# First-half inverse roots moved to GpSimd as one power, and the per-layer-embedding stage's first-half squares added on VectorE

## The reference

```
def rmsnorm(x, g):
    xf = x.astype(jnp.float32)
    y = xf * lax.rsqrt(jnp.mean(xf * xf, axis=-1, keepdims=True) + EPS)
    return (y * g.astype(jnp.float32)).astype(x.dtype)
...
def conv_ffn(xn, w_up, conv_w, conv_b, w_down, prev):
    u = xn @ w_up
...
    return h @ w_down, up[:, -(CONV_W - 1):]

def ple_term(h, p, g, w_gate, w_proj):
    return jax.nn.sigmoid(rmsnorm(h, g) @ w_gate) * (p @ w_proj)
...
        hp = hp + rmsnorm(yp, g_post_mix[i])
        fp, cvp = conv_ffn(rmsnorm(hp, g_pre_ffn[i]), ffn_w_up[i], ffn_conv_w[i], ffn_conv_b[i], ffn_w_down[i],
                           jnp.zeros((Bp, CONV_W - 1, 2 * D_FF), hp.dtype))
        hp = hp + rmsnorm(fp, g_post_ffn[i])
        hp = hp + ple_term(hp, p_prompt[i], g_ple[i], ple_w_gate[i], ple_w_proj[i])
```

## Time and profile before

| | us |
|---|---|
| median of 3 runs | 1319.02 |
| lowest, highest | 1319.0, 1319.26 |
| the profiled execution | 1319.47 |
| its span | 1317.7 |
| TensorE busy | 1307.0 |
| VectorE busy | 856.8 |
| ScalarE busy | 583.8 |
| GpSimd busy | 67.8 |

### The profile page before, as it was taken

How to read it: one execution, slowest core, us unless ns; L and a number is a source line. 1 busy time by engine, 2 the same in 40 slices (tenths; PEclk the granted TensorE clock), 3 DMA queues, 4 the chain that set the end, 5 groups by cost and what they waited for, 6 DMA issues and landing times.

```text
span 1317.7 us, 25501 instructions
## 1 busy us (share of the span) xinstructions
PE 1307.0 (99%) x10944; PEld 1270.2 (96%) x10944; DVE 856.8 (65%) x1552; ACT 583.8 (44%) x1031; POOL 67.8 (5%) x102
## 2 busy tenths in 40 slices
PE   9999999999999999999999999999999999999998
PEld 7999989999999999999999987999999999999998
DVE  6437675887777775222887788698777777432385
ACT  5222345654444443222754768554444444222371
POOL 1110322000000000000013010000000000000000
PEclk9999999999999999999999999999999999999999
DMA  4542732213332233222414232221332233322231
GB/s 169 174 107 93 244 113 65 97 57 89 96 97 85 93 96 134 89 89 83 145 33 150 87 101 70 80 83 41 96 97 86 91 97 98 122 89 89 77 129 65
DMA packets 34802, 131.64 MB, mean 100 GB/s; under 512 B 4197, under 2 KB 4781, under 8 KB 34401
## 3 DMA queue, kind: packets, MB, share of 16 engines
q1 hardware_dynamic: 29376, 111.59, 26.2%
q0 software_dynamic: 5024, 18.05, 4.4%
q10 hardware_dynamic: 288, 0.37, 0.1%
HBM read 121.08 MB, written 10.05 MB: 100 GB/s over the span
## 4 chain that ended last, share of the span: by engine, by line
PE 94%; DVE 3%; ACT 1%; DMA 1%; issue 0%; SPq 0%; DVEq 0%; ACTq 0%
PE tile L1151 24%; PE tile L1155 24%; PE tile L1153 24%; PE tile L1161 4%; PE tile L1162 4%; PE tile L1163 4%; PE tile L1665 1%; PE side L1161 1%; DVE wL L1848 1%; DMA h<-in_x 1%; PE side L1162 1%; PE side L1163 1%; DVE cv L1881 0%; DVE cg L1853 0%; PE side L1323 0%
## 5 line engine op out<-in xcount | busy, mean ns | idle before, releaser
L734 ACT ACTIVATE wH<-raw 128x1024 fp32r<-128x1024 f32 (+1 forms) x191 | 212.0, 1112 | 379.7 <-DMA raw<-in_w_up 142.0
L1151 PE MATMUL tile<-xH,wH 128*128 128x260 f32 x1800 | 365.0, 284 | 2.5 <-DVE xL L1942 1.5
L1155 PE MATMUL tile<-xH,wL 128*128 128x260 f32 x1800 | 362.7, 283 | 0.0
L1153 PE MATMUL tile<-xL,wH 128*128 128x260 f32 x1800 | 362.2, 283 | 0.0
L1848 DVE TENSOR_TENSOR wL<-raw,wH 128x1024 fp32r<-128x1024 f32 (+1 forms) x191 | 248.1, 1300 | 152.1 <-ACT wH L734 147.9
L1151 PEld LDWEIGHTS tile<-xH,wH 128*128 128x128 f32 x1800 | 277.3, 189 | 6.7 <-DVE kvq L1896 2.6
L1155 PEld LDWEIGHTS tile<-xH,wL 128*128 128x128 f32 x1800 | 277.5, 188 | 0.0
L1153 PEld LDWEIGHTS tile<-xL,wH 128*128 128x128 f32 x1800 | 276.7, 188 | 0.0
L1896 DVE SCALAR_TENSOR_TENSOR u<-tile,rstd 128x520 f32<-128x520 f32 x96 | 67.2, 700 | 123.4 <-PE tile L1155 123.4
L1151 PE MATMUL tile<-hidH,wH 128*128 128x260 f32 x616 | 124.3, 283 | 0.0
L1155 PE MATMUL tile<-hidH,wL 128*128 128x260 f32 x616 | 123.8, 282 | 0.0
(11 more groups left out here) (461 smaller groups left out, 1895.1 us busy)
## 6 DMA issues: line engine op xcount, KB each, us to landing
raw<-in_w_up SPq DMA_DIRECT2D x88, 512.0 KB, 3.6
raw<-in_w_down SPq DMA_DIRECT2D x32, 704.0 KB, 4.1
raw<-in_w_ple SPq DMA_DIRECT2D x16, 512.0 KB, 5.7
raw<-in_w_qo SPq DMA_DIRECT2D x12, 512.0 KB, 3.5
raw<-in_w_qkv SPq DMA_DIRECT2D x12, 512.0 KB, 3.6
raw<-in_w_kv SPq DMA_DIRECT2D x11, 512.0 KB, 3.6
cring<-in_c_in POOLq DMA_DIRECT2D x8, 512.0 KB, 4.6
out_c_s<-cring POOLq DMA_DIRECT2D x8, 512.0 KB, 3.2
```

The costliest lines, as they stand in the source:

```text
L734: nc.scalar.activation(wH[j][:, 0:n], raw[j][:, 0:n], ACT.Copy).then_inc(s_high, 1)
L1151: nc.tensor.matmul(out[:, q, 0:HT], wh, x[0][:, k, tokens(q)], start=first, stop=False)
L1153: nc.tensor.matmul(out[:, q, 0:HT], wh, x[1][:, k, tokens(q)], start=False, stop=False)
L1155: mm = nc.tensor.matmul(out[:, q, 0:HT], wl, x[0][:, k, tokens(q)], start=False, stop=last)
```

## The change

There are three edits, in both layers.

1. For the first half of "up" and of "ple", ScalarE writes mean square plus epsilon (the identity in place of the root), and GpSimd raises it to the power -0.5 in place, against a one-column constant. VectorE's reciprocal of this half is gone; VectorE waits for GpSimd.
2. The first half of "ple" has no column groups: TensorE's two `square_group` calls and ScalarE's `group_sums` go. VectorE adds the 8 tiles of squares in four instructions (`fold_early`, `fold_late`), and `square_sum` moves from before the first halves to after the fifth k of the third one.
3. The order in "ple" follows: VectorE's three weight blocks stand earlier, ScalarE splits the third block before its third input of the second half, `pre_root` stands one input later, and TensorE's groups for the second half stand one k later.

```
-GROUPED = {sq: n + 1 for n, sq in enumerate(sq for sq in PREROOT if sq[0][:2] != "up" or sq[1])}
+GROUPED = {sq: n + 1 for n, sq in enumerate(sq for sq in PREROOT if sq[1])}
...
+            def inverse_root(stage):
+
+                pool.wait_ge(s_rinv, PREROOT[stage, 1] // 2)
+                pool.wait_ge(s_rootp, PREROOT[stage, 0])
+                nc.gpsimd.tensor_tensor(rstd[:, tokens(0)], rstd[:, tokens(0)], minus_half[:].to_broadcast([P, HT]), ALU.pow
+                                        ).then_inc(s_rinv, 1)
+
             for layer in range(NL):
...
                 nc.gpsimd.memset(u[:, :, 0:2], 0.0).then_inc(s_pad, 1)
+                inverse_root(up)
                 pool.wait_ge(s_hid, FT * (layer + 1))
                 pool.dma_start(g.newrows[layer], newrows[:]).then_inc(s_out, 16)
                 stored += 1
 
                 pool.dma_start(pin[:], g.p[layer]).then_inc(s_p, 16)
+                inverse_root(ple)
...
-                nc.scalar.activation(rstd[:, tokens(q)], sums[:, q, 0:HT], ACT.Sqrt, bias=eps[:, 0:1],
+                nc.scalar.activation(rstd[:, tokens(q)], sums[:, q, 0:HT], ACT.Sqrt if q else ACT.Identity, bias=eps[:, 0:1],
...
                 ple_input(0, 1)
-                group_sums(ple, 0)
                 high(ple, 1)
                 p_copy(6)
                 ple_input(1, 1)
                 p_copy(7)
+                high(ple, 2)
                 ple_input(2, 1)
+                ple_input(3, 1)
                 pre_root(ple, 0)
-                ple_input(3, 1)
-                high(ple, 2)
...
-                    if j == 2:
-                        square_group(ple, 0, 0)
-                    if j == 5:
-                        square_group(ple, 0, 1)
 
                 yd = YREAD0[down]
-                square_sum(ple, 0)
                 first_half(ple, 0, (s_yr, yd + KT - 1))
                 first_half(ple, 1, (s_pwr, 2 * KT * (layer + 1)))
-                first_half(ple, 2, (s_pwr, 2 * KT * (layer + 1)))
-                for k in range(3):
+                first_half(ple, 2, (s_pwr, 2 * KT * (layer + 1)), lambda k: square_sum(ple, 0) if k == 4 else None)
+                for k in range(4):
...
             def pre_one_over(stage, q):
+                if q == 0:
+                    dve.wait_ge(s_rinv, 1 + PREROOT[stage, 1] // 2)
+                    return
...
+            def fold_early(stage):
+
+                dve.wait_ge(s_sq, SQ0[stage] + KT // 2)
+                chain.did(nc.vector.tensor_tensor(sg[0], sg[0], sg[1], ALU.add))
+
+            def fold_late(stage):
+
+                dve.wait_ge(s_sq, SQ0[stage] + KT)
+                late = squares_ple[:, 0:KT // 2, :].rearrange("p n t -> p (n t)")
+                chain.link(nc.vector.tensor_tensor(late[:, 0:T], late[:, 0:T], late[:, T:2 * T], ALU.add))
+                chain.link(nc.vector.tensor_tensor(sg[0], sg[0], late[:, 0:T], ALU.add))
+                nc.vector.tensor_tensor(square(stage, 0, 0), square(stage, 0, 0), square(stage, 0, 1), ALU.add).then_inc(s_fold, 1)
...
+                    if k == KT:
+                        fold_early(ple)
                 one_over(down, 1, cg[:, tokens(1)])
+                low(ple, 0)
                 for k in range(KT + 2):
                     step(k, 1)
-                    if k in (1, 3, 5):
-                        low(ple, k // 2)
+                    if k in (2, 3):
+                        low(ple, k - 1)
+                    if k == 3:
+                        fold_late(ple)
```

More of the change, by code:

```diff
@@ L193, in build @@
         const = sb("const", [P, C_ALL])
-        eps = sb("eps", [P, 1])
+        eps_half = sb("eps_half", [P, 2])
+        eps, minus_half = eps_half[:, 0:1], eps_half[:, 1:2]
         touch = sb("touch", [P, 1])
@@ L331, in build @@
         s_psum, s_psumr = sem("pre_squares_by_group"), sem("pre_squares_by_group_read")
-        s_fold = sem("pre_squares_added")
+        s_fold, s_rinv = sem("pre_squares_added"), sem("pre_root_inverted")
         s_raw0, s_high0, s_low0 = sem("first_weights_in"), sem("first_weights_high"), sem("first_weights_low")
@@ L620, in _ @@
             nc.gpsimd.memset(eps[:], EPS).then_inc(s_eps, 1)
+            nc.gpsimd.memset(minus_half[:], -0.5).then_inc(s_rinv, 1)
             nc.gpsimd.memset(kst[:].bitcast(F32), 0.0).then_inc(s_zero, 1)
@@ L1210, in square_sum @@
                     pe.wait_ge(s_root, ROOT[POST[stage], q])
-                    pe.wait_ge(s_fold, int(stage[2]) + 1)
+                    pe.wait_ge(s_fold, PREROOT[stage, 1] // 2)
                 nc.tensor.matmul(sums[:, q, 0:HT], ones, square(stage, q, 0), start=True, stop=True).then_inc(s_squ, 1)
@@ L1619, in feed_forward @@
                 square_group(ple, 1, 1)
+                for c in range(2):
+                    second_half(ple, c, 4, 5)
+                square_sum(ple, 1)
+                second_half(ple, 2, 4, 5)
                 for c in range(SPLIT):
[L1621 to L1624, removed]
+                    second_half(ple, c, 5, KT)
                 for c in range(SPLIT, KT):
```

## The result

The changed kernel takes 1456.72 us, the median of 4 runs (1455.89 to 1457.53), against 1319.08 us for 4 runs of the kernel before (1319.0 to 1319.26): 1.1041 times as long, 95% interval 1.1028 to 1.1054. That is 137.6 us slower, where 2.2 us faster was forecast, and far above the range (1315.8 to 1328). The profiled execution has a span of 1455.0 us.

The account below looks back on a forecast made before the run. TensorE, busy 99% of the span, was taken as the bound; gains of 0.44 us (up) and 0.65 us (ple) in each of two layers, 2.2 us, off 1319.02 gave 1316.8 us, range 1315.8 to 1328.

Parts of the forecast that it names:

- The power's own time: Length of GpSimd's power on 260 columns: about 3 us, between ends of 0.6 and 32 us.
- Rival A: Power outlasts its cover, VectorE and TensorE's chunk 3 wait: 2 x (P - 6.3) on 1316.8; chance 0.21 beyond 8.8 us.
- the sum: Total gain over both layers' up and ple stages: 2 x (0.44 + 0.65) = 2.2 us.
- The gain of 0.44 us in the up stages and 0.65 us in the ple stages: Per layer, chunk 3 starts earlier: 0.44 us in up by VectorE's dropped reciprocal, 0.65 in ple.
- Rival D: Freed 1.5 us all turn into waits for copies and adds: 1319.0; shares 0.12 with powers of 6.3 to 8.8 us.
- The new wait before chunk 1 for the p copies: In ple, TensorE waits for ScalarE's last copies of the p product: a new gap of 1 us.
- Rival C: TensorE is not held by the p copies: up to 1.99 + 0.44 us gained a layer, 1314.2; chance 0.08.
- The covers: Power length that stays hidden before VectorE needs the inverse: 10.3 us in up, about 6.3 us in ple.
- The ports: GpSimd's two-input power takes about 0.4 us from VectorE, however long it computes.
- Rival B: VectorE is held for the power's whole length: 1323.3 us at a power of 3 us; chance 0.09.

Follow-up runs that it names:

- experiment 7: The changed kernel with the power over the first 64 columns alone, the other columns left without an inverse root: 1329.98 us, ratio 1.0081.
- experiment 2: The changed kernel with GpSimd multiplying by -0.5 in place of raising to -0.5: 1316.97 us, ratio 0.9982.
- the probe: The kernel before with seven more GpSimd instructions, a multiply and six powers, in an idle stretch on an unused buffer: 1319.18 us.

## Why the prediction was wrong

**The step that failed is "The power's own time".** It put P at "about 3 us", by the ratio of VectorE's reciprocal to its add, between the ends 0.6 and 32. P is 41.84 us: fourteen times the value taken, and beyond the end that I had called the one from above. Two things were wrong in it. The upper end came from instructions of another operation, with 8 columns of bf16: 0.97 us each, spread over 8 columns. Such a row tells what small instructions of that kind cost; it bounds no other operation's cost per column. The power on 8 columns takes 1.64 us. And the ratio of 4.1 was carried from one engine to another, as if the same work were hard to the same degree on both: on GpSimd the power is 41.87 / 0.62 = 68 times the multiply. With ends of 0.6 and 32 us and a cover of 6.3, most of the interval lay on the losing side. I still gave that side 0.21 and cut the range at P = 11.9. The price by the upper end itself, 2 x (32 - 6.3) = 51 us, was worked out in no rival.

**Rival A is what happened,** but its price was too small in three ways. It was worked out for P = 10. It counted the ple stages alone, though beyond 10.3 + 1.4 = 11.7 us the up stages pay as well. And it left out the clock behind the wait: 1.5, 2.8, 2.0 and 1.5 us in the table, some 2.4 in experiment 7. With P = 41.84 the waits are 2 x (41.84 - 6.3) = 71.1 us in the ple stages and 2 x (41.84 - 11.7) = 60.3 us in the up stages; less the 2.2 of the sum and plus the 7.8 of these four for the clock they make 137.0. Measured were 137.6, and 137.3 between the spans.

**What held.**
- The gain of 0.44 us in the up stages and 0.65 us in the ple stages: with the power's length out of the way, 2.3 us faster against 2.2 forecast (experiment 2). The markers of that trace, counted from "up"'s start, give 0.5 us for each up stage and 0.64 for each ple stage, and its timeline shows no wait of TensorE before chunk 3 of "up", where 0.53 us stood. Rival D, by which nothing of it shows, is out too. In the changed kernel itself the wait before chunk 3 of "ple" is 35.33 and 0.15 for the restart, 35.48, while the markers moved by 34.86: 0.62 us gained.
- The new wait before chunk 1 for the p copies, forecast at 1 us and shown at 683.10 as 0.75 us, 0.9 with its restart. Rival C, which denied it, is out.
- The covers: 6.3 us in the ple stage (5.45 us free, 10.56 us costs 4.2 us of waiting), 10.3 in the up stage until the first read, with the 1.4 us behind it that I had named as a wait for the second root but not counted as cover.
- The ports: about 0.4 us from VectorE, however long the power computes; 0.37 were measured beside 0.61 us and beside 41.84 us, and 0.41 in the probe. It isn't simply proportional to the columns: in experiment 7 the row beside the start of 64 columns took 0.52 us in place of 0.48. In the up stage nothing was lost: the power starts there beside a reciprocal, which has one input, and the rows behind it keep their 0.48 us. Rival B, with VectorE held for the whole length, is refuted: the rows at 689.95 and 690.28 keep their 0.42 and 0.48 us under a power that runs until 730.96. The Trainium skill's rule of an exclusive lock for the whole instruction (SBUF — State Buffer, Who interferes with whom) is not what this trace shows: only the row that started with GpSimd's instruction was slowed.

**What stays open.** Why a power costs 0.16 us a column, and how the work is spread over partitions, no run tells; only that it isn't one by one. Why the clock costs 1.5 us behind one wait of 35.33 us and 2.8 behind the other stays open as well.

## What to carry to other kernels

An operation whose price no row shows is the first thing to bound, and only a row of the same operation on the same engine bounds it from above: compare the widest end with the cover before the gain is summed up, and if most of the interval lies beyond the cover, forecast the loss. An inverse root that ScalarE writes itself costs what the root does and takes the reciprocal off VectorE; look for such a merged operation before a step is handed to a third engine. Its accuracy is a question of its own, which no row here answers. A wait of several us on TensorE costs more than its length, since the clock behind it is low for a while; waits under 1 us here did not.

## What the runs showed of the hardware

- The power on GpSimd: 0.16 us per column of fp32, 41.80 to 42.04 us for 260 columns on 1, 8, 16 or 128 partitions, up to 4% more by value; a multiply of the same shape 0.62 us.
- A VectorE instruction with two inputs in SBUF lost 0.37 to 0.41 us when it started with a two-input GpSimd instruction of 260 columns, whether that took 0.61 or 41.84 us. Those that started later beside the same power lost nothing: 0.42 and 0.48 us at 689.95 and 690.28, 1.22 to 1.23 us for 27 weight blocks in the probe.
- TensorE, after standing idle for 30.41 us, ran with a granted clock of 0.50, the 1.2 GHz level, in the 3.3 us read behind the wait, and then at 0.98 and 1.00. After an idle of only 4.04 us the clock was 0.75 on average over 10 us, as it was over 12 us behind 35.33 us. The two waits of 30.41 us cost 1.5 and 2.0 us by the clock, the two of 35.33 us 2.8 and 1.5, that of 4.04 us 2.4: the short wait cost as much as the long ones. Waits of 0.53 to 0.77 us left the clock at 1.00.
- ScalarE's reciprocal square root of 128x260 out of PSUM took 0.48 us, as its square root did; VectorE's reciprocal took 1.77.
